# A two-block transformer kernel in float32 on one NeuronCore: weight blocks woven column by column, stationary operands read with a step of two

## The reference, cut to what matters

```python
z  = einsum("bsd,dn->bsn", h, w_in)          # 1024 -> 4608          ("in")
y_b, y_a = s @ w_b_out, a @ w_a_out          # 512 -> 1024 each      ("b_out", "a_out")
x += (g_a * y_a + g_b * y_b) @ w_o           # 1024 -> 1024          ("o")
u  = h @ w_up;  x += f @ w_down              # 1024 -> 5632, 2816 -> 1024 ("up", "down")
x += sigmoid(rmsnorm(x) @ w_ple_gate) * (p @ w_ple)                # ("gate", "ple")
proj = h @ w_in_2;  x += rms_norm(mix @ w_out_2)                   # ("in2", "out2")
u  = h2 @ w_up_2;   x += rms_norm(f2 @ w_down_2)   # 1024 -> 8192, 4096 -> 1024 ("up2", "down2")
```

## Time and profile before

| | |
|---|---|
| time, median of 3 runs | 753.13 us (753.06 to 756.38) |
| span of the profiled execution | 753.8 us |
| PE busy | 744.0 us, 99% of the span |
| PE weight loads busy | 723.4 us, 96% |
| DVE busy | 577.9 us, 77% |
| ACT busy | 452.2 us, 60% |
| POOL busy | 210.7 us, 28% |
| bytes moved by DMA | 135.48 MB, mean 180 GB/s |

### The profile page before, as it was taken

The page is one execution under the profiler, slowest core; times in us unless marked ns, Lnnn a source line. Parts: engine busy times, 40 slices in busy tenths (PEclk is TensorE's granted clock), DMA queues, the critical chain, the costliest instruction groups (busy, mean ns, idle before and its releaser), DMA issues.

```text
span 753.8 us, 16764 instructions
## 1 busy us (share of the span) xinstructions
PE 744.0 (99%) x5950; PEld 723.4 (96%) x5950; DVE 577.9 (77%) x1049; ACT 452.2 (60%) x765; POOL 210.7 (28%) x136
## 2 busy tenths in 40 slices
PE   8999999999999999999999999999999999999997
PEld 8999999999999999999999999899999999988885
DVE  6999977877887887434887794899999999973333
ACT  7645555556665665444765697876766666643431
POOL 0476743460000000343464002422122122212220
PEclk9999999999999999999999999999999999999999
DMA  8575644565555567644443333355565555666551
GB/s 313 177 238 178 196 155 137 188 207 190 189 184 182 191 200 246 204 161 141 163 165 130 124 130 128 107 195 196 195 194 184 182 192 192 205 217 195 184 179 56
DMA packets 37917, 135.48 MB, mean 180 GB/s; under 512 B 4464, under 2 KB 4720, under 8 KB 37872
## 3 DMA queue, kind: packets, MB, share of 16 engines
q1 hardware_dynamic: 37728, 134.86, 54.3%
q10 hardware_dynamic: 144, 0.00, 0.0%
HBM read 133.80 MB, written 1.05 MB: 179 GB/s over the span
## 4 chain that ended last, share of the span: by engine, by line
PE 72%; DVE 5%; ACT 3%; issue 2%; POOL 1%; DMA 1%; DVEq 0%; POOLq 0%; SPq 0%; ACTq 0%
PE bank L1901 20%; PE bank L1903 19%; PE bank L1902 19%; PE bank L2348 4%; PE bank L2347 4%; PE bank L2349 4%; DVE w_lo L1223 2%; ACT w_hi L787 1%; DMA raw<-in_w_o 1%; POOL X L755 1%; PE bank L2176 1%; ACT score L1079 0%; PE bank L2200 0%; DVE sumsq L1813 0%; DVE score L1730 0%
## 5 line engine op out<-in xcount | busy, mean ns | idle before, releaser
L1901 PE MATMUL bank<-h_hi,w_hi 128*128 128x256 f32 x1372 | 386.6, 282 | 1.6 <-DVE h_lo L1235 0.8
L1902 PE MATMUL bank<-h_lo,w_hi 128*128 128x256 f32 x1372 | 383.4, 279 | 0.0
L1903 PE MATMUL bank<-h_hi,w_lo 128*128 128x256 f32 x1372 | 382.6, 279 | 0.0
L787 ACT ACTIVATE w_hi<-raw 128x1024 fp32r<-128x1024 f32 (+2 forms) x243 | 258.6, 1067 | 94.3 <-PE bank L1903 42.4
L1223 DVE TENSOR_TENSOR w_lo<-raw,w_hi 128x1024 fp32r<-128x1024 f32 (+2 forms) x187 | 235.9, 1264 | 88.4 <-ACT w_hi L787 86.4
L1901 PEld LDWEIGHTS bank<-h_hi,w_hi 128*128 128x128 f32 x1372 | 257.8, 188 | 3.2 <-DVE w_lo L1301 1.0
L1902 PEld LDWEIGHTS bank<-h_lo,w_hi 128*128 128x128 f32 x1372 | 257.9, 188 | 0.0
L1903 PEld LDWEIGHTS bank<-h_hi,w_lo 128*128 128x128 f32 x1372 | 257.9, 188 | 0.0
L636 POOL TENSOR_TENSOR w_lo<-raw,w_hi 128x1024 fp32r<-128x1024 f32 (+1 forms) x56 | 139.0, 2485 | 384.8 <-ACT w_hi L787 376.3
L1281 DVE TENSOR_TENSOR bank<-bank,scales 128x256 f32<-128x256 f32 x116 | 49.4, 429 | 27.4 <-PE bank L1903 21.0
L1572 DVE SCALAR_TENSOR_TENSOR cg<-bank,vec,cg 128x255 f32<-128x255 f32 x108 | 51.2, 474 | 0.7 <-ACT cg L1019 0.6
(11 more groups left out here) (235 smaller groups left out, 948.6 us busy)
## 6 DMA issues: line engine op xcount, KB each, us to landing
raw<-in_w_up SPq DMA_DIRECT2D x108, 512.0 KB, 4.2
raw<-in_w_in SPq DMA_DIRECT2D x53, 512.0 KB, 3.9
raw<-in_w_down SPq DMA_DIRECT2D x32, 512.0 KB, 4.2
raw<-in_w_down SPq DMA_DIRECT2D x16, 704.0 KB, 4.1
raw<-in_w_o SPq DMA_DIRECT2D x8, 512.0 KB, 4.6
raw<-in_w_gate SPq DMA_DIRECT2D x8, 512.0 KB, 3.3
raw<-in_w_out SPq DMA_DIRECT2D x8, 512.0 KB, 3.3
raw<-in_w_b_out SPq DMA_DIRECT2D x4, 512.0 KB, 3.5
```

The lines of the kernel that those rows point to most:

```text
L787: nc.scalar.activation(hi_of(u)[:, cols], raw[s][:, cols], ACT.Copy).then_inc(hi_ready, 1)
L1901: nc.tensor.matmul(ps, wh, hi[:, k, :], start=start and n == 0, stop=False)
L1902: nc.tensor.matmul(ps, wh, lo[:, k, :], start=False, stop=False)
L1903: last = nc.tensor.matmul(ps, wl, hi[:, k, :], start=False, stop=stop and n == len(ks) - 1)
```

## The change

On the host, two neighbouring blocks of a unit are interleaved: column 0 of block 0, column 0 of block 1, column 1 of block 0, and so on. An odd last block (block 10 of a "down" unit) stays as it was. On the core, a product's stationary operand is no longer 128 neighbouring columns (512 bytes of a partition) but every second column of 255 (1,020 bytes), from the pair's first column for an even block and from its second for an odd one. The column step in bytes goes from 4 to 8. The weights of down2 are not woven. The moving operands, the transfers, the rounding, the waits and the order of instructions on every engine are the same.

```diff
+        def stationary(tile, k, blocks=DC):
+
+            if k + 1 == blocks and blocks % 2:
+                return tile[:, k * P:(k + 1) * P]
+            first = k // 2 * 2 * P + k % 2
+            return tile[:, first:first + 2 * P - 1:2]
...
             def products(ps, s, block0, ks, hi, lo, start, stop, ready=None, w=None, blocks=DC):
...
-                    wh, wl = (part[:, b * P:(b + 1) * P] for part in w_of)
+                    wh, wl = (stationary(part, b, blocks) for part in w_of)
...
             def lagging(tiles, ks, hi, lo, hi_here, lo_here, start, stop):
...
-                            wh, wl = (part[s][:, k * P:(k + 1) * P] for part in (w_hi, w_lo))
+                            wh, wl = (stationary(part[s], k) for part in (w_hi, w_lo))
...
             def rounded_first(u):
...
-                    wh = w_hi[slot(u)][:, k * P:(k + 1) * P]
+                    wh = stationary(w_hi[slot(u)], k)
...
 def units_of(w, k_blocks, order=None):
...
     t = t.reshape(-1, k_blocks, P, P).transpose(0, 2, 1, 3)
-    return t.reshape(-1, P, k_blocks * P)
+    count, pairs = t.shape[0], k_blocks // 2
+    woven = t[:, :, :2 * pairs].reshape(count, P, pairs, 2, P).swapaxes(3, 4)
+    return np.concatenate([woven.reshape(count, P, -1), t[:, :, 2 * pairs:].reshape(count, P, k_blocks % 2 * P)], axis=2)
```

More of the change, by code:

```diff
@@ L1891, in unit_here, with products @@
                 pe.wait_ge(lo_ready[slot(u)], it + (u // RING + 1))
-            def products(ps, s, block0, ks, hi, lo, start, stop, ready=None, w=None):
+            def products(ps, s, block0, ks, hi, lo, start, stop, ready=None, w=None, blocks=DC):
                 w_of = w or (w_hi[s], w_lo[s])
@@ L1919, in lagging @@
                         for ps, s in tiles:
-                            last = nc.tensor.matmul(ps, w_hi[s][:, behind * P:(behind + 1) * P],
+                            last = nc.tensor.matmul(ps, stationary(w_hi[s], behind),
                                                     lo[:, behind, :], start=False,
@@ L2020, in rounded_first @@
                 for k in range(DC):
-                    last = nc.tensor.matmul(ps, w_lo[slot(u)][:, k * P:(k + 1) * P], h2_hi[:, k, :],
+                    last = nc.tensor.matmul(ps, stationary(w_lo[slot(u)], k), h2_hi[:, k, :],
                                             start=False, stop=k == DC - 1)
@@ L2136, in down_tile @@
                     products(bank[slot(t)][:, 0:TOK], slot(u), 0, range(k * r, k * r + k),
-                             f_hi, f_lo, r == 0, r == per_tile - 1, ready).then_inc(unit_done, 1)
+                             f_hi, f_lo, r == 0, r == per_tile - 1, ready, blocks=k
+                             ).then_inc(unit_done, 1)
             for i in range(DC):
```

## The result

The changed kernel takes 770.87 us in the median (770.59 to 771.74, 4 runs), the kernel before 753.23 us beside it: a ratio of 1.0229 with a 95% interval from 1.0216 to 1.0242. It is 17.6 us slower where I had forecast 22 us faster.

A forecast was written before the change was run, and what follows sets the result against it. PE's pace was taken as the bound; savings by phase of 4.3 + 2.1 + 6.4 + 2.9 + 1.0 + 1.5 + 4.4 = 22.6 us took 753.8 to 731.2, given as 731. Range 716 to 807 us, likeliest case 716 to 746.

The forecast's parts named there:

- What bounds the kernel: Whole kernel: PE, busy 99% of the span, sets the time; products take 116.6 to 117.8 ns where 106.7 are needed.
- The load by itself: Weight loads of the 5,184 woven products: a step of two takes the same time as before, 108.8 to 111.7 ns.
- The meeting of the two reads: Stationary and moving reads in SBUF: at equal speeds they stop delaying each other, pace 111.7 ns, saving 4.9 or 6.1 per product.
- The excess: Every product: 10.0 to 11.1 ns over 106.7 with 256 moving columns, 13.4 with 512, read as one read waiting.
- More meetings, slower: Rival, woven products: waits go with bytes crossed, so the excess doubles, 53.5 us more, 807 us; chance 0.20.
- The doubled load: Rival, woven weight loads: a load takes 218 to 223 ns and becomes the pace, 1,278 to 1,303 us; chance 0.12.
- VectorE's cap in up2: Phase up2: DVE, busy 166.6 of 171.0 us, becomes the bound, so 4.4 us of the 7.5 us saving count.

The follow-up runs named there:

- before_past0: The kernel before with the weight ring tiles at a multiple of 64 bytes instead of 32 past one: 768.1 us, ratio 1.0188.
- second probe: Kernel before plus groups of 24 to 96 constant-data products ahead of its work, varying starts and steps; 256 columns, step one: 113.3 to 120.0 ns per product.
- first probe: Kernel before plus 46 groups of 24 constant-data products ahead of its work; 192 moving columns: 111.7 ns at step one, 118.3 at step two.
- before_at0: The kernel before with ring tiles at 0 modulo 256 bytes, activations at 192, down2's weights stored 48 columns on: 743.5 us, ratio 0.9856.
- third probe: Constant-data products ahead of the kernel's work, varying starts and moving columns; 4 moving columns at step two: 117.5 ns per load.
- before_rel64: The kernel before with ring tiles at 0 modulo 128 bytes, activations staying at 64 modulo 128: 760.1 us, ratio 1.0091.

## Why the prediction was wrong

**What bounds the kernel** was right: PE's pace sets the time, and a change of 3.4 ns in it is paid in full over 5,184 products. So was the warning that only 5 to 8 ns of slack hide a slower load, and that down2 would stay at 226.7 ns.

**The load by itself** is the step that failed. I wrote "The bounds are the same time (108.8 to 111.7) and twice that. I take the same", on the ground that durations grew by only 8 ns from a step of zero to a step of one. That comparison couldn't tell: up to a step of one the column count bounds a load, at 111.7 ns with either step, and the price of memory, 1.82 to 1.85 ns for each new 16 bytes, lies hidden below it. At a step of two it comes to the surface, at 118.3 ns. The rows of before could have warned, not told. A stationary read with a step of two goes over as many bytes as the moving read of 256 columns, whose product takes 116.6 ns; had all of that been the moving read's own price, the load would have come out at about 117. But 512 and 256 moving columns differ by only 110.1 ns, and by that measure the load would have stayed at 111.7.

The Trainium skill's rule on cachelines ("SBUF — State Buffer", the note on cachelines), which I cited for a free step of two, asks for at least two hits per line. The runs agree that one hit is dear (232.9 ns, double), and find two hits not quite free: 6.6 ns on 111.7.

**The meeting of the two reads.** The observation on the earlier trace rows was right and held up in the whole kernel: a shift of 32 bytes costs 1.9% (before_past0). The conclusion from it, "Then they either never meet, or meet once, wait once and are apart for good", was wrong. With a stationary read of 118.3 ns beside 256 moving columns, the pace settles at 120.0 ns for most starts and never below 118.3. So of the 3.4 ns that a product lost, the slower load explains 1.7. Why the pace is 120.0 and not 118.3 was not shown; there is no slack left in either read to catch up in, but that is only an argument.

**The excess** of 10 ns over 106.7 was read as waits of one read for the other. The probes show only the part between 113.3 and 120.0 to go with the starts, and none of it below 113.3. With a stationary read that stays on one column (line 1928 of the second probe) the pace is still 5.62/48 = 117.1 ns, so a stationary read that goes through memory isn't needed for an excess. What makes it isn't settled. It can be the moving read's own price per 16 bytes: 116.6 is 64 x 1.82, and 320, 384 and 512 moving columns in the first probe, `still` 32 bytes on, settle at 146.7, 173.3 and 233.3 ns, 1.83, 1.81 and 1.82 per 16 bytes. It can in part be an addition to each product, as the prediction had it: 146.7, 173.3 and, with both starts alike, 226.7 ns for 512 are each 13.3 ns over what the prediction takes for these columns at 2.4 GHz. Taking the excess as avoidable is what made the gain of 22.6 us look possible.

**The rivals.** The third, "More meetings, slower", ended on the right side, and its chance of 0.20 was too small, but its mechanism is not the one: a doubled excess would be 106.7 + 20.0 = 126.7 ns and 53.5 us, and 120.0 to 121.0 ns and 17.6 us came. The doubled load (0.12) has the mechanism nearly right, a price per fetch of memory, and a wrong size at this step: it is what a step of four does.

**VectorE's cap in up2** had no part in the result, and before_at0 comes up to it without settling it. Busy time from 510 to 660 us of that kernel, with VectorE third:

```profile
510.00:660.00 150.00, 150.00 (x1308) 149.31 (x1307) 149.86 (x266) 104.86 (x168) 33.73 (x14) 1.00 0.59 199
```

At 113.4 ns per product VectorE is busy 149.9 of 150 us; it had 2.6% to spare, and the pace fell by 2.7%. But 113.3 ns is also the lowest pace of the probe, where VectorE waits, so whether VectorE holds PE up there isn't shown.

## What to carry to other kernels

In these runs a float32 weight load paid about the larger of two prices: its columns (0.87 ns each) and its 16-byte pieces of memory (1.8 ns each). A moving operand with a step of two paid 1.8 ns per piece as well. Before changing an access step, work out both for both operands: a read that had slack in the one can lose it in the other, and here the slack was smaller than it looked. Where products run at 113 to 120 ns for the same shapes, try the start of the weight tiles modulo 256 bytes before anything else; here it was worth 25 us between the best and the worst of four places, and 10 us over the kernel before.

## What the hardware showed that I had not expected

- The price per 16 bytes doesn't go with PE's clock. In the second probe a step of four stands once in a stretch where the granted clock is at its lower level (1.2 GHz), and in the first probe once at the higher (2.4 GHz). Busy time by stretch, with the granted clock as the third number from the end, first of the second probe, then of the first:

```profile
76.50:81.50 5.00, 5.00 (x24) 5.00 (x23) 0.00 (x0) 0.00 (x0) 0.00 (x0) 0.50 0.00 0
```

```profile
112.00:117.00 5.00, 5.00 (x23) 5.00 (x23) 0.00 (x0) 0.00 (x0) 0.00 (x0) 1.00 0.00 0
```

  The settled pace is 233.3 ns in both, while a step of one needs 213.3 ns at the lower level (64 moving columns) and 111.7 at the higher. In the first probe PE was at full pace by its neighbours too, whose 256-column products ran at 120 ns.
- A moving operand with a step of two (256 columns, 128 pieces of 16 bytes) took 229.6 ns per product in the first probe, nearly the 226.7 of 512 neighbouring columns.
- The same products with the same addresses can run at 113.3 or at 117.8 ns for as long as a phase lasts, and at 116.6 or 117.8 ns in the kernel before. The last pair makes some 1.9 us over the 1,584 products of up and down, most of the 2.4 us between the two spans of the kernel before.
- With 512 moving columns the start matters too: 226.7 ns where both operands start alike modulo 256, 233.3 in most other places, in the third probe as in before_rel64's down2 (233.3).
